# Scatter products of a mixture-of-experts stage, moved behind the second weight product in some couples of experts

## The reference

```python
def grouped_moe(x, router_w, router_bias, w_gate, w_up, w_down):
    ...                                   # gates: top 2 of 4 experts of the best group, normalised
    def step(acc, ew):
        g_e, wg_e, wu_e, wd_e = ew
        h = jax.nn.silu(x2 @ wg_e) * (x2 @ wu_e)
        return acc + (h @ wd_e) * g_e[:, None].astype(x2.dtype), None
    out, _ = lax.scan(step, jnp.zeros_like(x2), (gates.T, w_gate, w_up, w_down))
```

## Time and profile before

| | us |
|---|---|
| median of 3 runs | 1286.13 (1285.0 to 1289.55) |
| the profiled execution | 1284.22 |
| its span, first to last instruction | 1282.5 |

### The profile page before, as it was taken

One profiled execution on the slowest core, in us unless ns is written; L12 is line 12 of the kernel. 1 busy time (PEld: TensorE's weight loads), 2 busy tenths in 40 slices (PEclk: granted clock), 3 DMA queues, 4 the chain that ended last, 5 costly groups with the idle time before them and its releaser, 6 DMA issues.

```text
span 1282.5 us, 16097 instructions
## 1 busy us (share of the span) xinstructions
PE 1196.0 (93%) x6536; PEld 855.8 (67%) x6536; DVE 641.8 (50%) x949; ACT 477.8 (37%) x741; POOL 205.3 (16%) x190
## 2 busy tenths in 40 slices
PE   7998999999988998999999989989999789999998
PEld 7986754344435986744444336879887676888996
DVE  3897631212115678711222125694389884545544
ACT  3496421011103566211111013465566433434442
POOL 6000000000002000000000000185788451000000
PEclk9999989999999999799999998999999899999999
DMA  9900879999998540889999994433344331364450
GB/s 333 326 1 1 346 294 430 426 429 427 428 413 283 190 145 26 339 368 428 427 429 426 427 376 152 144 131 132 132 149 178 126 138 66 131 229 165 175 219 33
DMA packets 68162, 321.23 MB, mean 250 GB/s; under 512 B 4071, under 2 KB 12660, under 8 KB 55418
## 3 DMA queue, kind: packets, MB, share of 16 engines
q1 hardware_dynamic: 64944, 308.57, 60.8%
q0 software_dynamic: 2592, 11.42, 2.5%
q10 hardware_dynamic: 554, 0.23, 0.1%
HBM read 317.02 MB, written 3.18 MB: 250 GB/s over the span
## 4 chain that ended last, share of the span: by engine, by line
PE 69%; DVE 17%; ACT 5%; DMA 5%; issue 3%; POOL 1%; DVEq 0%; SPq 0%; ACTq 0%
PE bank L1527 31%; PE bank L1710 23%; PE bank L1592 4%; PE bank L1701 3%; DMA arena<-in_moe_w_up_dram 2%; DMA ring<-in_w_kv_dram 2%; PE bank L1759 2%; DVE w_lo L666 2%; POOL w_lo L666 1%; PE bank L1495 1%; ACT w_hi L953 1%; DVE arena L2292 1%; DVE rows L2846 1%; DVE arena L2865 1%; PE bank L1599 1%
## 5 line engine op out<-in xcount | busy, mean ns | idle before, releaser
L666 POOL TENSOR_TENSOR w_lo<-ring,w_hi 128x512 fp32r<-128x512 f32 (+1 forms) x124 | 176.6, 1455 | 668.8 <-ACT w_hi L953 668.8
L953 ACT ACTIVATE w_hi<-ring 128x2048 fp32r<-128x2048 f32 (+1 forms) x102 | 192.0, 1883 | 218.6 <-PE bank L1527 217.1
L666 DVE TENSOR_TENSOR w_lo<-ring,w_hi 128x2048 fp32r<-128x2048 f32 x71 | 160.8, 2266 | 150.6 <-ACT w_hi L953 150.1
L1527 PE MATMUL bank<-x_hi,w_hi 128*128 128x256 f32 x672 | 111.7, 289 | 3.8 <-DVE x_lo L2247 2.2
L1527 PE MATMUL bank<-x_hi,w_lo 128*128 128x256 f32 x672 | 108.7, 284 | 0.8 <-POOL w_lo L666 0.7
L1527 PE MATMUL bank<-x_lo,w_hi 128*128 128x256 f32 x672 | 108.3, 284 | 0.0
L1527 PE MATMUL bank<-w_hi,x_hi 128*128 128x512 f32 (+1 forms) x336 | 95.9, 400 | 9.4 <-DVE x_lo L2627 3.6
L1710 PE MATMUL bank<-arena 128*64 128x512 f32 x352 | 98.6, 594 | 1.9 <-ACT arena L953 1.8
L1527 PE MATMUL bank<-w_lo,x_hi 128*128 128x512 f32 (+1 forms) x336 | 94.9, 398 | 4.8 <-POOL w_lo L666 4.7
L1527 PEld LDWEIGHTS bank<-x_hi,w_hi 128*128 128x128 f32 x672 | 92.9, 192 | 6.4 <-issue 5.9
L953 ACT ACTIVATE arena<-bank 128x512 f32<-128x512 f32 (+3 forms) x85 | 40.0, 486 | 146.2 <-PE bank L1743 103.9
(11 more groups left out here) (333 smaller groups left out, 1779.0 us busy)
## 6 DMA issues: line engine op xcount, KB each, us to landing
ring<-in_w_in_dram SPq DMA_DIRECT2D x15, 2048.0 KB, 8.0
ring<-in_moe_w_gate_dram SPq DMA_DIRECT2D x12, 2048.0 KB, 19.8
arena<-in_moe_w_down_dram SPq DMA_DIRECT2D x12, 2048.0 KB, 21.6
arena<-in_moe_w_gate_dram SPq DMA_DIRECT2D x12, 2048.0 KB, 17.3
ring<-in_moe_w_down_dram SPq DMA_DIRECT2D x12, 2048.0 KB, 18.3
ring<-in_moe_w_up_dram SPq DMA_DIRECT2D x12, 2048.0 KB, 17.5
arena<-in_moe_w_up_dram SPq DMA_DIRECT2D x12, 2048.0 KB, 21.3
wslots<-in_moe_w_up_dram SPq DMA_DIRECT2D x8, 2048.0 KB, 22.4
```

The source lines that it names most:

```text
L666: last = ops.tensor_tensor(part(w_lo, label, hb)[:, x].bitcast(F32R), ring_half(label, hb)[:, x], part(w_hi, label, hb)[:, x], ALU.subtract)
L953: return s.activation(dst, src, ACT.Copy)
L1527: last = mm(bank(use_)[:, at:at + cols], still, moving, start=start and opens and (hb, n, k) == (0, 0, 0), stop=stop and closes and (hb, n ...
```

## The change

In the couples u = 2, 4, 6 and 7 `scatter(u - 1)` is issued behind the up product and behind `selected(u + 1)`, directly in front of `hidden_T(u)`. VectorE's `scattered(u - 1)` moves with it: behind the product `hx`, in front of `picked(u + 1)`. Couples 1, 3 and 5 stay as they are. No instruction is added or removed, and the banks and buffers are the same. There are 14 scatters ahead of the last one of a layer in the two layers, and 8 of them move.

```diff
@@ TensorE @@
                 for u in range(PAIRS):
                     into("gate", u)
-                    if u:
+                    late = u and u % 2 == 0 or u + 1 == PAIRS
+                    if u and not late:
                         scatter(u - 1)
                     if u % 2 and u + 1 < PAIRS:
                         gathered((u + 1) // 2, 0)
                     into("up", u)
                     if u + 1 < PAIRS:
                         selected(u + 1)
+                    if late:
+                        scatter(u - 1)
                     ahead_ = u % 2 and u + 1 < PAIRS
@@ VectorE @@
-                    if u:
+                    late = u and u % 2 == 0 or u + 1 == PAIRS
+                    if u and not late:
                         scattered(u - 1)
                     freed(dve, ("gate", l, u))
                     freed(dve, ("selT", l, u))
                     ...
                     free(v.scalar_tensor_tensor(hidden_rows(hx[:, 0, :]), by_hidden(sg[:, 0, :]),
                     ...
+                    if late:
+                        scattered(u - 1)
                     if u + 1 < PAIRS:
                         picked(u + 1)
```

## The result

| | before | after |
|---|---|---|
| median, 7 runs each | 1286.13 us (1284.29 to 1289.55) | 1294.96 us (1292.17 to 1297.05) |
| the profiled execution | 1284.22 us | 1294.96 us |
| mean granted clock | 0.976 | 0.968 |

The ratio of the runs is 1.0053, 95% interval 1.0038 to 1.0068, that is 6.8 us (4.9 to 8.7); the two medians lie 8.8 us apart. The prediction was wrong: 7 to 9 us slower where 1.2 were forecast, and outside the range.

What follows compares the result with a forecast made beforehand. Transfers were taken to bound the expert stage up to the last up product; 0.3 and 0.7 us, and 0.1 twice, made 1.2 us later: 1285.4 profiled, 1287.3 us as median, range 1284.5 to 1290.8.

Steps and rivals of the forecast that it cites:

- What bounds the kernel: Expert stage: transfers set the pace up to couple 7's up product, which waits 0.63 us; afterwards TensorE's and VectorE's chain counts.
- only as a rival: Cover before couple 7's up product fails, or the `w_kv` transfer lands later: 1289.2 to 1289.7 us, chance 20%.
- The chain in couples 2, 4 and 6: VectorE's additions now precede the selection copy, so transposes come 0.9 us later each, 2.7 us per layer (1.9 to 3.75).
- The cover: Couple 7, before the up product: 2.07 us of moved scatter and 0.63 us of transfer wait hide 2.7 us per layer.
- Couple 7: Transposes behind the scatter come 0.7 us later: all counts in layer 1, 0.3 us in layer 0, where 0.4 is hidden.
- The clock: TensorE's granted clock in the expert stages: assumed held at 1.00 through the waits, with no term in the sum.
- The sum: Whole kernel: 0.3 and 0.7 us, and 0.1 twice, 1.2 us later (1.0 to 3.1), with no clock term.
- the rival that had it: Clock falls at six waits around the transposes, 4 us lost each: 24 us, 1310 us, chance 6%.
- The first reason: Against a clock fall: outside the gaps around the transposes TensorE is busy without a break for some 20 us.
- The second: Against a clock fall: it stayed 1.00 through gaps of 1.07 and 0.88 us, and 1.96 us before the last scatter.
- The skill's rule for the change: Keep TensorE busy: filling its 1.07 us wait before the transposes in six places would be a gain, 1279.7 us, chance 4%.

Runs made afterwards that it cites:

- e7: Changed kernel with waits of couples 2, 4 and 6 filled to size: two constant matmuls before the transposes, one behind; 1286.77 us, ratio 1.0002 against the kernel before.
- e3: Changed kernel, but in couples 2, 4 and 6 VectorE copies the selection first and makes its additions behind that; 1286.34 us, ratio 0.9992 against the kernel before.
- e1: Kernel before with only the moves in couples 2, 4 and 6, couple 7 as before; 1299.72 us, ratio 1.0109.
- e2: Kernel before with only the move in couple 7; 1286.61 us, ratio 0.9991.
- e8: Kernel before, one constant matmul in front of and one behind the transposes in couples 0, 2, 4, 6 and 7; 1285.59 us, ratio 0.9994.
- e11: Second set of the kernel before with one constant matmul on each side of the transposes in couples 0, 2, 4, 6 and 7; 1285.49 us, ratio 0.9985.

## Why the prediction was wrong

- **What bounds the kernel.** Right for the kernel before: with the clock held, the delays of the even couples ended in front of the last up product (e7, e3). It ceased to hold in the changed kernel, whose last up product finds its transfer landed; I had seen that only as a rival.
- **The chain in couples 2, 4 and 6.** Right. Predicted: additions from 242.70 to 245.2, transposes 0.9 us late, a wait of about 2 us, released by the copy. Measured: 0.75 us late, 2.07 us. The scatter started 241.47, the first addition 0.75 us behind it; between the last addition and the copy the timeline has 0.23 us of idle time against my 0.13 (0.0 to 0.45).
- **The cover.** Right in size: 2.9 us were taken back in couple 7 of layer 1 against my 2.7, and without it the even couples alone cost more, though part of that is a further fall (e1).
- **Couple 7.** 0.7 us in layer 1 and 0.3 in layer 0 predicted; 0.5 and 0.1 measured in the profile, no net cost in the runs (e2). The 0.4 us that I had hidden in layer 0 were hidden.
- **The clock.** Here it failed. The sum put the clock at nothing, and the rival that had it got a chance of 6%. The first reason was that TensorE is busy without a break for some 20 us outside these gaps. By the rows it is busy even longer, some 50 us from one even couple's waits to the next one's, and the clock fell all the same (from 571.8 to 620.8 us in layer 1, then the fall at 623). The second was that one profile held the clock through the waits of 1.07 and 0.88 us, and through 1.96 us in front of the last scatter. That profile was one draw: in couple 0 of layer 1 the clock fell in the profile after with waits of 1.05 and 0.89 us, and behind the wait of 1.96 us in front of the last scatter the clock fell in the profiles of both e8 and e11. What the change makes is 2.07 us, followed after 0.66 us of transposes by another 0.89 us, and of these two the rival weighed only the first, against the 1.96 us; in the profiles the long falls of the couples came only where both stood unfilled. What decides whether a given wait lets the clock fall stays open: the clock held through the same 2.07 us in couples 4 and 6 of layer 0. The rule of the Trainium skill, TensorE: Matmul & The Clock Gate, "HAM oscillation — how this bites in real kernels", that waits between bursts of matmuls throttle the clock anew, agrees in direction with what came, at 0.50 behind 623 us; not every one of these waits did it.
- **The size of that rival.** 24 us for six falls of 4 us; measured 2.8 us for a long fall and 1.6 for a short one, and five of them in the profile, three long and two short, one of these in a couple that the change leaves alone. Part of a long fall runs over the wait behind the transposes, where it costs nothing, and the cover takes some 2.7 us of the sum of delays and falls per layer.
- **The skill's rule for the change**, Perfetto Trace Analysis, Optimization Strategies, to keep the matmul engine as busy as possible: by my reading of it the change was a gain, and that was further off than my sum; e3, where TensorE does wait less for VectorE, saved nothing either, as its wait for transfers shows. But idle time had a second price. The change made the wait in front of the transposes longer, 2.07 us for 1.07, and read by that the rule pointed the right way.

## What to carry to other kernels

Before moving work out of the time beside a product and into a chain between two products, look at TensorE's idle time over the whole place and not only at its longest wait, and count the clock as part of the price even where the engine isn't the bound; here 1 us more of idle time and 0.75 us of delay at each of six places cost 7 to 9 us, none of which the same delays cost with the clock held (e7). If a wait can't be removed, matmuls of constants into an idle bank, sized from a measured row to be shorter than the wait, can hold the clock at no measurable cost; the clock can still fall at a wait left unfilled (e8, e11). A profile in which the clock was held in a place doesn't say that it always is: look at the spread of the runs too.

## What the runs showed of the hardware that I had not expected

- The clock fell behind idle stretches of 1.05 and 0.89 us with 0.66 us of transposes between (couple 0, layer 1, after), and was held through the same stretches in other couples and other kernels. The code of that place is the same in the kernel before, whose profile held.
- In front of the last scatter of layer 0 the clock held through a wait of 1.96 us in the profile before, and fell behind one of 1.96 and 1.97 us in those of e8 and e11, where TensorE had been idle less ahead of it.
- The falls in the expert stages came in two lengths: some 3.4 us (568.4 to 571.8, costing 1.6 us) and some 6.8 us (623.0 to 629.9, costing 2.8).
- A float32 matmul of 512 columns from the `fill` helper counts as two instructions and takes 0.86 us at full clock (3.43 us for four), which the count of eight in the timeline shows:

```profile
244.00 3.59 PE L1774 MATMUL bank<-blockmask,ident 128*128 128x512 f32 x8
247.43 0.60 PE L1743 MATMUL bank<-ident,arena 128*128 128x128 f32 x4
```
